# Kernel of three blocks in 32-bit floats on one core: norms by column groups, the output projection's pooling half between them, and a new order in two attentions

## What is computed

```python
for l in range(2):                                   # first block
    x = layer_norm(ALPHA*x + hybrid_mixer(x, ...))   # latent attention (8 heads) beside a convolution branch:
                                                     #   31 taps, layer norm over 512 channels, swish
    x = layer_norm(ALPHA*x + cross_attention(x, mem))# 4 heads of 256, 256 memory tokens
    x = layer_norm(ALPHA*x + swiglu(x))
# second block
h = rmsnorm(x)*(1+scale)+shift
q, k, v = silu(short_conv(h @ w_in))                 # k, v also for 256 context tokens
q, k = l2norm(q)*128**-0.5, l2norm(k)                # 4 heads of 128
o = gated delta rule in both directions, chunks of 64
o = rmsnorm(o, dn_norm) * silu(gate)                 # by head
pooled = pool_mixer(...)*pool_scale                  # 512 features
x = x + g1 * (concat([o, pooled]) @ w_out)
x = x + g2 * expert_choice_ffn(modulate(rmsnorm(x))) # 16 experts, 64 tokens each
out = rmsnorm(x)
```

## Time and profile before

| | us |
|---|---|
| median of 3 runs | 2781.04 (2780.64 to 2784.96) |
| the profiled execution, its own time | 2781.38 |
| its span in the profile | 2779.6 |
| PE busy | 2578.7 (93%) |
| DVE busy | 1247.0 (45%) |
| ACT busy | 717.8 (26%) |
| POOL busy | 152.8 (5%) |
| DMA, mean over the span | 137 GB/s |

### The profile page before, as it was taken

How to read it: one execution, slowest core, us unless ns; L and a number is a source line. 1 busy time by engine, 2 the same in 40 slices (tenths; PEclk the granted TensorE clock), 3 DMA queues, 4 the chain that set the end, 5 groups by cost and what they waited for, 6 DMA issues and landing times.

```text
span 2779.6 us, 33532 instructions
## 1 busy us (share of the span) xinstructions
PE 2578.7 (93%) x14414; PEld 1677.2 (60%) x14414; DVE 1247.0 (45%) x1919; ACT 717.8 (26%) x1146; POOL 152.8 (5%) x102
## 2 busy tenths in 40 slices
PE   8989999999999989999999998996888779999997
PEld 4446677888884446767888884554777434444332
DVE  5962546433347952636434342536545441221122
ACT  2243343322221342433223222124212131001111
POOL 0000000000000000000000004401323010000000
PEclk9999999999999999999999998988999899999999
DMA  4234212324322243212333324010000228999997
GB/s 151 87 122 151 91 61 61 93 78 112 87 73 93 87 152 136 76 61 61 106 87 102 96 65 145 31 61 32 2 2 3 91 91 324 421 421 421 421 421 299
DMA packets 243386, 380.56 MB, mean 137 GB/s; under 512 B 21769, under 2 KB 182822, under 8 KB 218534
## 3 DMA queue, kind: packets, MB, share of 16 engines
q1 hardware_dynamic: 242876, 378.08, 38.0%
q10 hardware_dynamic: 362, 0.33, 0.0%
HBM read 376.28 MB, written 2.10 MB: 136 GB/s over the span
## 4 chain that ended last, share of the span: by engine, by line
PE 82%; DVE 8%; DMA 6%; ACT 3%; issue 1%; SPq 0%; DVEq 0%; ACTq 0%
PE banks L1013 32%; PE banks L948 10%; PE banks L1741 9%; PE banks L1392 8%; PE banks L1511 4%; PE banks L996 2%; DMA arena<-in_w_gate 2%; DMA arena<-in_w_up 2%; PE banks L1282 1%; PE banks L1000 1%; DMA ring<-in_w_gate 1%; PE banks L1687 1%; PE banks L1052 1%; PE banks L1258 1%; DVE arena L2909 1%
## 5 line engine op out<-in xcount | busy, mean ns | idle before, releaser
L2004 ACT ACTIVATE w_hi<-ring 128x2048 fp32r<-128x2048 f32 (+1 forms) x100 | 174.6, 1746 | 424.0 <-PE banks L1013 424.0
L2499 DVE TENSOR_TENSOR w_lo<-ring,w_hi 128x2048 fp32r<-128x2048 f32 (+1 forms) x96 | 198.7, 2069 | 150.1 <-ACT w_hi L2004 148.8
L1013 PE MATMUL banks<-ffn_x_hi,w_hi 128*128 128x512 f32 x640 | 249.0, 389 | 0.0
L1013 PE MATMUL banks<-ffn_x_lo,w_hi 128*128 128x512 f32 x640 | 249.0, 389 | 0.0
L1013 PE MATMUL banks<-ffn_x_hi,w_lo 128*128 128x512 f32 x640 | 249.0, 389 | 0.0
L2623 DVE SCALAR_TENSOR_TENSOR arena<-arena,taps 128x512 f32<-128x512 f32 x240 | 166.1, 746 | 2.5
L2825 DVE TENSOR_TENSOR squares<-gates,banks 128x512 f32<-128x512 f32 x44 | 30.3, 688 | 275.5 <-PE banks L1013 262.3
L1392 PE MATMUL banks<-zT,ring 128*128 128x512 f32 x320 | 144.9, 611 | 2.5 <-ACT zT L2131 1.7
L948 PE MATMUL banks<-xT,ring 128*128 128x512 f32 x320 | 139.1, 594 | 0.5 <-ACT taps L1880 0.5
L1013 PE MATMUL banks<-ffn_hidden_hi,w_hi 128*128 128x512 f32 x352 | 138.4, 393 | 0.0
L1013 PE MATMUL banks<-ffn_hidden_hi,w_lo 128*128 128x512 f32 x352 | 137.1, 389 | 0.0
(11 more groups left out here) (443 smaller groups left out, 4344.2 us busy)
## 6 DMA issues: line engine op xcount, KB each, us to landing
ring<-in_ffn_w_in SPq DMA_DIRECT2D x88, 512.0 KB, 5.1
ring<-in_w_down SPq DMA_DIRECT2D x30, 1024.0 KB, 24.0
arena<-in_w_gate SPq DMA_DIRECT2D x29, 1024.0 KB, 23.9
arena<-in_w_up SPq DMA_DIRECT2D x29, 1024.0 KB, 23.2
ring<-in_w_gate SPq DMA_DIRECT2D x26, 1024.0 KB, 22.8
ring<-in_w_up SPq DMA_DIRECT2D x26, 1024.0 KB, 23.6
arena<-in_w_down SPq DMA_DIRECT2D x26, 1024.0 KB, 25.5
ring<-in_w_mod SPq DMA_DIRECT2D x24, 1024.0 KB, 6.9
```

Of the source, the lines that this page charges most:

```text
L1013: mm = pe.matmul(bank[:, :], weights(wp, k), rhs(rp, k), start=(k == 0 and wp == rp), stop=(k == n - 1 and wp == 1))
L2004: nc.scalar.activation(hi[:, 0:m], raw[n % 2][:, 0:m], ACT.Copy).then_inc(f_hi.sem, 1)
L2499: ins = V.tensor_tensor(lo[:, 0:m], raw[n % 2][:, 0:m], hi[:, 0:m].bitcast(F32), ALU.subtract)
```

## The change

In words:

- Convolution norm: PE sums the squares with `by_tokens`, ACT and DVE work on 128 columns, PE spreads the reciprocal into bank 5 after `values(6)`, and the four multiplications on DVE come after the last head.
- Cross attention: ACT copies head 0's turned probabilities first, then `high`, then head 2's exponentials; the products with the values use four banks instead of two.
- Norms of q and k: sums by groups of columns (192 or 128 wide), root and reciprocal of that width, spread on PE, multiplications with the bank. ACT's and DVE's work on the decays comes ahead of this loop, the decays' products share bank 5, the pooling copies come ahead of silu of the gate.
- Heads' norms: the same form, two heads at a time; the output projection's tiles 0 to 3 start with the products of the pooling half (k = 4 to 7), which need no norm; two of them come before the heads' sums, one before each pair of spreads. The k loop is outside for the other half.
- The norm behind it: sums by column groups, two after each of tiles 4 to 7, reciprocal of 128 columns, spread.

```diff
@@ PE, latent attention
-                        mm = pe.matmul(ps[3][:, :], ones, (squares, gates)[t // 2][:, t % 2, :], start=(t == 0),
-                                       stop=(t == CT - 1))
-                        mm.then_inc(cvar.sem, 1)
+                        by_tokens(3, (squares, gates)[t // 2][:, t % 2, :], t == 0, t == CT - 1).then_inc(cvar.sem, 1)
...
+                    if h == HEADS - 2:
+                        pe.wait_ge(mod_in.sem, mod_in.at(l, MOD_CHUNKS))
+                        pe.wait_ge(cmul.sem, cmul.at(l, 1))
+                        spread(5, std[:, 2 * P:3 * P]).then_inc(cvar.sem, 1)
@@ PE, cross attention
+                    if h == 1:
+                        pe.wait_ge(xs_exp.sem, xs_exp.at(l, 12))
...
-                        if n >= 2:
-                            pe.wait_ge(xo_ev.sem, xo_ev.at(l, n - 1))
+                        if n >= 4:
+                            pe.wait_ge(xo_ev.sem, xo_ev.at(l, n - 3))
@@ PE, norms of q and k
+            def tokens_sum(out, src, n, start, stop):
+
+                for j in range(4):
+                    mm = pe.matmul(out[j * 32:(j + 1) * 32, 0:n], ones[:, 0:32], src[:, j * n:(j + 1) * n], start=start, stop=stop)
...
+            def l2_spread(i):
+                pe.wait_ge(l2_rec, i + 1)
+                if i >= 2:
+                    pe.wait_ge(l2_ok, i - 1)
...
-                mm = pe.matmul(ps[b][:, :], ones, pre[:, i % 2, 0:S], start=True, stop=True)
-                say_spent(mm)
-                mm = pe.matmul(ps[b + 1][:, 0:CTX], ones, pre[:, i % 2, S:S + CTX], start=True, stop=True)
-                mm.then_inc(l2_mm, 1)
+                n = l2_cols(i)
+                tokens_sum(ps[(5, 7)[i % 2]], pre[:, i % 2, 0:4 * n], n, True, True).then_inc(l2_mm, 1)
+                if i >= 1:
+                    l2_spread(i - 1)
+            l2_spread(2 * DH - 1)
@@ PE, end
+            arrived2(C_OUT2)
+            delta.wait(pe, "dve", NT - 1, "S1b")
+            for t in range(2):
+                out_product(t, range(DH, KT), ps[4 + t])
+            pe.wait_ge(delta.sem["dve"], delta.last("dve"))
             for h in range(DH):
...
+                head_sum(h)
+            out_product(2, range(DH, KT), ps[6])
+            head_spread(0)
+            head_spread(1)
+            out_product(3, range(DH, KT), ps[7])
+            pe.wait_ge(l2_std, 2 * DH + 2)
+            head_spread(2)
+            head_spread(3)
+            for k in range(DH):
+                pe.wait_ge(l2_ok, 2 * DH + k + 1)
+                for t in range(4):
+                    mm = out_product(t, [k], ps[4 + t])
...
+            for t in range(4, KT):
+                pe.wait_ge(wo_ok, t - 3)
+                out_product(t, [*range(DH, KT), *range(DH)], ps[t]).then_inc(wo_mm, 1)
+                if t == KT - 1:
+                    give_back(1)
+                rms_sum(2 * (t - 4))
+                rms_sum(2 * (t - 4) + 1)
+            pe.wait_ge(n_rec, 2)
+            for j in range(ST):
+                mm = pe.matmul(ps[1][:, j * P:(j + 1) * P], spreads[:, j * P:(j + 1) * P], std[:, 3 * P:4 * P], start=True, stop=True)
@@ ACT, cross attention
-                for h in range(2, XH + 2):
-                    if h < XH:
-                        xexps(h)
-                    xturned(h - 2)
+                xturned(0)
+                high(N_XO + 1)
+                xexps(2)
+                xturned(1)
+                xexps(3)
+                xturned(2)
+                xturned(3)
@@ ACT, norms of q and k: the decays' Exp, Exp, Ln, Sigmoid now come ahead of this loop
-            for i in range(2 * DH + 2):
+            for i in range(2 * DH + 1):
...
+                    A1(acc[:, m % 2, 0:n], ps[(5, 7)[m % 2]][:, 0:n], ACT.Sqrt, bias=eps[:, 1:2]).then_inc(l2_std, 1)
...
+            for i in range(4):
+                act.wait_ge(pl_mm, i + 1)
+                A1(mix2[:, DH + i, :], ps[pool_bank[i]][:, :], ACT.Copy, scale=par2[:, Q_PS + i:Q_PS + i + 1]).then_inc(pl_ev, 1)
             act.wait_ge(pj_ev, g)
             A1(gateT, gateT, ACT.Silu)
@@ DVE, latent attention, after the last head
+                dve.wait_ge(cvar.sem, cvar.at(l, CT + 1))
+                for t in range(CT):
+                    V.tensor_tensor(mixT[:, CT + t, :], mixT[:, CT + t, :], ps[5][:, :], ALU.mult).then_inc(cmul.sem, 1)
@@ DVE, norms of q and k
+                V.reciprocal(acc[:, i % 2, 256:256 + n], acc[:, i % 2, 0:n]).then_inc(l2_rec, 1)
...
+                dve.wait_ge(l2_sp, i + 1)
@@ DVE, end
+                V.reciprocal(head_dev[:, 2 + i, 0:2 * P], head_dev[:, i, 0:2 * P]).then_inc(l2_rec, 1)
...
+            V.reciprocal(std[:, 3 * P:4 * P], std[:, 2 * P:3 * P]).then_inc(n_rec, 1)
```

More of the change, by code:

```diff
@@ L1395, in product @@
                 return mm
-            def rms_sums(first, n=S):
-                for t in range(KT):
-                    pe.wait_ge(n_sq, first + t + 1)
-                    mm = pe.matmul(ps[1][:, 0:n], ones, squares[:, t % 2, 0:n], start=(t == 0), stop=(t == KT - 1))
-                    mm.then_inc(n_mm, 1)
             pe.wait_ge(ctx_out, KT)
@@ L1614, in _ @@
                     says("X", mm)
-            for h in range(DH):
-                pe.wait_ge(l2_sq, 2 * DH + h + 1)
-                if h == 0:
-                    pe.wait_ge(delta.sem["dve"], delta.last("dve"))
-                if h >= 2:
-                    pe.wait_ge(l2_std, 2 * DH + h - 1)
-                pe.matmul(ps[h % 2][:, :], ones, squares[:, h % 2, :], start=True, stop=True).then_inc(l2_mm, 1)
-            pe.wait_ge(l2_ok, 2 * DH + DH)
-            for t in range(KT):
-                c = C_OUT2 + t // 4
-                if t % 4 == 0:
-                    arrived2(c)
-                if t >= 4:
-                    pe.wait_ge(wo_ok, t - 3)
-                wo = w(c, 0, KT, 512)
-                mm = product(ps[4 + t % 4], lambda k: wo[:, k, (t % 4) * P:(t % 4 + 1) * P], lambda k: mix2[:, k, :])
-                mm.then_inc(wo_mm, 1)
-                if t % 4 == 3:
-                    give_back(1)
@@ L1638, in _, with out_product, head_sum @@
-            pe.wait_ge(wo_ok, KT)
-            rms_sums(4 + KT)
+            def out_product(t, ks, bank):
+                c = C_OUT2 + t // 4
+                wo = w(c, 0, KT, 512)
+                for k in ks:
+                    mm = pe.matmul(bank, wo[:, k, (t % 4) * P:(t % 4 + 1) * P], mix2[:, k, :], start=(k == DH), stop=(k == DH - 1))
+                    if k == DH:
+                        say_spent(mm)
+                return mm
+            def head_sum(h):
+                pe.wait_ge(l2_sq, 2 * DH + h + 1)
+                src = (squares, gates)[h // 2][:, h % 2, :]
+                tokens_sum(ps[h // 2][:, (h % 2) * P:(h % 2 + 1) * P], src, P, True, True).then_inc(l2_mm, 1)
@@ new lines, in head_spread @@
+            def head_spread(h):
+                pe.wait_ge(l2_rec, 2 * DH + h // 2 + 1)
+                for j in range(4):
+                    mm = pe.matmul(ps[(2, 3, 0, 1)[h]][:, j * P:(j + 1) * P], spreads[:, j * P:(j + 1) * P],
+                                   head_dev[:, 2 + h // 2, (h % 2) * P:(h % 2 + 1) * P], start=True, stop=True)
+                mm.then_inc(l2_sp, 1)
+            arrived2(C_OUT2)
+            delta.wait(pe, "dve", NT - 1, "S1b")
+            for t in range(2):
+                out_product(t, range(DH, KT), ps[4 + t])
@@ L1973, in _ @@
                         act.wait_ge(cvar.sem, cvar.at(l, CT))
[L1974 removed]
+                        nc.scalar.activation(std[:, 0:P], ps[3][:, 0:P], ACT.Copy, scale=1.0 / CW).then_inc(cstd.sem, 1)
                     if 1 <= h <= MOD_CHUNKS:
@@ L2864, in _ @@
                 V.tensor_tensor(zT[:, t, :], xT[:, t, :], ps[1][:, :], ALU.mult).then_inc(n_mul, 1)
-            def rms(src, dst):
-                dve.wait_ge(n_std, 3)
-                v = done(V.reciprocal(std[:, :], std[:, :]))
-                dve.wait_ge(vec2, v)
-                for t in range(KT):
-                    V.tensor_tensor(dst[:, t, :], src[:, t, :], std[:, :], ALU.mult).then_inc(n_mul, 1)
             V.memset(w_rt[:, :, NE:MOD_COLS], 0.0)
```

183 lines of the change are left out of this document (97 added, 86 removed).

## The result

The changed kernel takes 2734.88 us (median of 4 runs, 2732.3 to 2736.12), the kernel before 2782.3 beside it: a ratio of 0.9827, with an interval of 0.981 to 0.9844. So 47.4 us were gained where 62.7 were forecast, and the end of the range (2733) lies 1.9 us too low. The profiled execution took 2736.12, with a span of 2734.0.

What follows compares the result with a forecast made beforehand. The expert phase was taken as a DMA-bound block of fixed length, so time saved ahead counts fully. Terms 5.8 + 17.5 + 10.0 + 29.4 = 62.7 us gave 2718.3 us (2713 to 2725), whole range 2709 to 2733.

Steps and rivals of the forecast that it cites:

- What bounds the kernel: Expert phase is a DMA-bound block of fixed length, 443 us; time taken off the path ahead comes off one for one.
- The end: Delta rule's end to router: PE never waits, 21.6 us off up to the output projection's end and 7.8 behind, 29.4 together.
- Rival 4: Output projection: pooling half cannot run early because w_out or pooled tiles are late, 15.88 us come back: 2734; chance 0.04.
- Cross attention: Both layers: new copy order and banks remove PE's waits before the values, 8.3 and 9.2 us off, 17.5 together.
- Latent attention: Convolution norm, both layers: shorter reciprocal and root, multiplications off the path, a spread added; net 2.9 us a layer, 5.8 together.
- the shorter sums are at the loop's start, where DVE's maxima are the chain: nothing: Latent attention's convolution norm: sums by column groups shorten PE's work but bring no time, since DVE sets the pace there.
- Norms of q and k: Stretch up to step 0 and its exponential: delta rule 13.6 us earlier, less 1.1 and 2.5; net 10.0, bounds 7 and 12.5.
- Rival 2: Less gain: late reciprocals stop PE in the q and k loop, head copies late in cross attention: 2732; chance 0.13.
- 1.1 lost: Step 0 of the delta rule: silu and table loads before its exponential take 4.5 us where 3.4 passed.
- Rival 1: More gain: lower-clock stretches vanish in latent attention (2.4 us a layer) and norms of q and k (2.5): 2711; chance 0.13.
- Rival 3: Each ACT table load costs as much again as it shows, five new on the path, 6.4 us: 2725; chance 0.04.
- Rival 5: Slower: PE reaches the expert phase with less rest and is held at 1.2 GHz; up to 3161; chance 0.03.

Runs made afterwards that it cites:

- The control: The changed kernel run once more, unaltered, for a second profile of the same program: 2736.32 us, ratio 0.9825.
- the runs of single parts: Four kernels, each the kernel before with one part changed: end 2754.61, q and k norms 2778.37, cross attention 2767.89, latent attention 2780.78 us.

## Why the prediction was right or wrong

**What bounds the kernel: right.** The experts' first product came at 2259.33 instead of 2302.76, 43.4 us earlier, and the span is 45.6 shorter. The block is 2.2 us shorter than it was.

**The end: right, 28.3 of 29.4.** PE goes without a gap for 62.2 us, from 2153.64 to 2215.87; the sum had said 60.9. The products took 0.874 us each and not 0.86, which is 0.9 of the 1.3 (the prediction's own 7.03/8 is 0.88; 0.86 is that row from its start to the next one's, 6.87/8); the six sums that stand in pairs between full products took 1.7, not 1.4. From there to the router it is 6.3 us instead of 14.4 in the kernel before, the 7.8 of the forecast and 0.3 more. Rival 4 (pooling half late) is out.

**Cross attention: 15.1 of 17.5 in the trace, 15.6 alone.** The mechanism was right to the row: a wait of 0.25 us ahead of head 0's values, 0.34 ahead of head 1's, 1.1 more gained in layer 1. Two terms were mis-sized. The length before was read to the second output product (428.8) where the first is at 428.23, 0.6 a layer. And the new length was put at 22.6 from the last query product, where it is 23.3: transposes of 1.04 us, not 0.9, and short waits of 1.3 in all, not 1.0, make the 0.7.

**Latent attention: 4.0 of 5.8 in the trace, 2.7 alone.** The step that failed is "the shorter sums are at the loop's start, where DVE's maxima are the chain: nothing". The step asked only which engine ends last, and left out what the idling that the shorter sums make does to PE's clock. The sums did save nothing, but they left PE idle for 0.70, 0.76 and 0.48 us in a row of small products, and the clock fell for 1.1 to 1.4 us of them a layer. At head 4 the stall went from 3.00 to 1.34 us, as the reciprocal's 2.4 us less would have it; the products behind it are low in both kernels. The control brought only 2.0 in the two layers (its loop in layer 0 took 64.40, not 63.08), so part of the 4.0 is the execution's luck and the 2.7 is the better figure.

**Norms of q and k: 4.8 of 10.0 in the trace, 5.1 alone. This is the largest miss.** The first spread came where it was forecast: at 1868.6 before the gains ahead of it, and 1857.07 + 11.3 is 1868.4. Some luck is in that, since the terms written down add up to 1867.8. From there, against the forecast's own steps:

- **From the first spread to the last: 0.7 us too long, with two larger errors that nearly cancel.** The lower clock was charged 2.5 us and cost 3.0 at the first spread and gate product. Spreads and sums were priced from a stream, 0.9 and 1.3 for a spread, 0.23 and 0.33 for a sum. Alone between other products they take 1.0 to 1.1 and 1.4 to 1.5, and 0.35 to 0.50, from start to start: some 2.2 us more. But the forecast's 32.4 us also held 2.2 us of waits for reciprocals, and behind the first spread PE waited for one 0.26 us in all. Rival 2, which put the loss of this loop on late reciprocals, is out.
- **From the last spread to step 0: 7.0 us, not 6.0**, 1.0 more.
- **From step 0 on: the step that failed is "1.1 lost", the charge for silu ahead of step 0's exponential.** The delay was 1.0, but with it PE idled 1.78 us instead of 0.75, and the products behind ran low: 246.5 to 248.0 without that delay, 251.7 to 252.0 with it. **A wait of 1 us cost 2.7 to 4.5 us on top of itself.** Against the kernel before (247.2) it was 4.8 us where 1.1 had been charged: 3.7 of the 5.2 that are missing in this part.

The forecast did see where the kernel before had its low stretch. It lay behind PE's 15.28 us of idling, and the pooling products took 6.36 us there where they take 3.62 in the changed kernel. What it didn't ask is where the new idle slots would put one: the sign that it named, a silu that delays step 0 by more than 1.1 us, was not met, and the loss came behind it all the same.

**Rival 1 (more, because low stretches vanish)** saw the mechanism and had its sign wrong: the mean granted clock rose only from 0.969 to 0.973, with low stretches back in dense products at the first spread, at step 0 and at head 0.

**Rival 3 (dearer table loads): out.** The rows show a load of 1.28 us and the activation right behind it, at 1900.95 and at 1904.16. The Trainium skill, "ScalarE: Activation LUTs", What ACT_TABLE_LOAD costs, adds a drain of 1.38 us to each switch; no gap in these rows leaves room for it, and the measurement decides. The other place of doubt, the change of tiling mode, is small at most: two sums of one tile side by side take 0.46 us (2160.71 to 2161.17), one alone 0.35, and a spread between two sums takes 1.09 against 0.89 each in a pair between full products, so 0.1 to 0.2 us each time. The Trainium skill, "TensorEngine Tiling (Array Packing)", Key Properties, has the engine drain at such a change, and that would fit. No run here separates it from another cost of starting a group.

**Rival 5 (slower by the clock): the right cause with the wrong place.** It looked for the lower level in the expert phase, after dense work, where the window shows 0.99. The argument against it, that the clock falls only after idling, held in that phase but not everywhere: the block of narrow products ran at a granted clock of 0.50 with no idle time in the trace. And I didn't turn it round: each wait that the change leaves or makes in front of dense products can cost more than its own length.

**The sum.** Of the 15.3 us missing, the runs of single parts account for 10.5 (rounded one by one): 4.9 in the norms of q and k, 3.1 in the latent attention, 1.9 in the cross attention, 0.5 at the end. The other 4.8 stay open. The profiled execution had 3.7 us of low clock at the feed-forward that the control hadn't, but the medians differ by as much in both sets of runs (47.4 and 47.9), so that doesn't explain them. Of the signs that the prediction named, the experts' first product came at 2259.33 and not near 2240, and step 0 at 1899.74 and not near 1884. The chance of 0.94 for "faster" was well placed. The range was not: its slow end, 2733, was made of late reciprocals and copies (rival 2), which didn't come, and lies within 2 us of the measured time by luck. No rival charged the clock behind a wait that the change leaves or makes.

## What to carry to other kernels

When you price a wait in front of dense products on TensorE, add the time that the products behind it take at the lower clock: here a wait of 1 us cost 3.7 to 5.5, and taking 3 us away gave 6. Look at the lengths of equal rows behind an idle slot and at the granted clock of the window, in the kernel before, and ask of each idle slot that the change leaves whether the next products are dense. A slot that can't be closed can be filled with products that nobody reads, as long as they end before what PE waits for: that gave 14.4 us here without touching the work, and a shorter operation on PE can lose time where it only makes the slot longer.

## What the runs showed of the hardware that was not expected

- PE ran at the lower level behind two idle slots of 1.64 and 1.72 us within 5 us (granted clock 0.69 from 337 to 348 us of the control). With the slots cut to 0.35 and 0.42 us the level stayed at the full clock (1.00 from 342.75 to 348 us, first product 0.47 us instead of 0.77).
- In unchanged code the low stretch comes in some executions and not in others: 371.65 and 367.92 us for the same feed-forward in two executions of one program. A profile of a single execution can be 4 us off by that.
- A block of 48 products with 16 columns ran with no idle time in the trace, and its last 32 at the lower level (granted clock 0.50): 0.43 us from start to start, where the first 16 of the changed kernel took 0.22. Spread among wide products, each added 0.22 us to the stream at a granted clock of 1.00.
